# The hid of experts 8 to 14 turned by VectorE instead of TensorE, and the final rows' loads, means and squares placed anew

## The reference

```python
aff = jax.nn.softmax((xf @ w_router).astype(jnp.float32), axis=-1)
cap = EC_CAPACITY_FACTOR * n // N_EXPERTS
gate, idx = lax.top_k(aff.T, cap)
xe = xf[idx]
hid = jax.nn.silu(jnp.einsum('ecd,edf->ecf', xe, w_gate)) * jnp.einsum('ecd,edf->ecf', xe, w_up)
ye = jnp.einsum('ecf,efd->ecd', hid, w_down) * gate[..., None].astype(h.dtype)
y = jnp.zeros_like(xf).at[idx.reshape(-1)].add(ye.reshape(-1, D))
...
x = x + gate2 * rmsnorm(y, g_post_ffn)
```

## Time and profile before

| what | value |
|---|---|
| median of three runs | 2362.34 us (2360.07 to 2362.45) |
| the profiled execution, its own time | 2362.63 us |
| its span | 2360.9 us |
| TensorE's matmuls busy | 2255.7 us, 96% |
| VectorE, ScalarE, GpSimd busy | 1349.1, 1100.5, 730.6 us |
| mean DMA rate | 217 GB/s |
| granted clock of TensorE, mean | 0.988 |

### The profile page before, as it was taken

How to read it: one execution, slowest core, us unless ns; L and a number is a source line. 1 busy time by engine, 2 the same in 40 slices (tenths; PEclk the granted TensorE clock), 3 DMA queues, 4 the chain that set the end, 5 groups by cost and what they waited for, 6 DMA issues and landing times. The chain is left out here.

```text
span 2360.9 us, 34620 instructions
## 1 busy us (share of the span) xinstructions
PE 2255.7 (96%) x13219; PEld 1876.9 (79%) x13219; DVE 1349.1 (57%) x1995; ACT 1100.5 (47%) x1782; POOL 730.6 (31%) x770
## 2 busy tenths in 40 slices
PE   6999999999999999999984999999999999999997
PEld 4679989867899898677763888888888888888885
DVE  3212344555422436665557877777777667677665
ACT  4212434555534436665542544544444455545552
POOL 3004241434233515340003222221222333443634
PEclk9999999999999999999996999999999999999998
DMA  8745445657554459764538666766667678988785
GB/s 314 265 114 184 153 148 192 188 137 185 139 188 152 148 172 247 225 183 162 169 128 313 215 218 231 248 223 224 209 224 244 229 267 316 334 311 302 286 304 178
DMA packets 224095, 511.49 MB, mean 217 GB/s; under 512 B 38420, under 2 KB 129444, under 8 KB 204496
## 3 DMA queue, kind: packets, MB, share of 16 engines
q1 hardware_dynamic: 174576, 394.78, 49.3%
q0 software_dynamic: 49376, 114.78, 16.5%
HBM read 415.32 MB, written 93.69 MB: 216 GB/s over the span
## 5 line engine op out<-in xcount | busy, mean ns | idle before, releaser
L2553 DVE TENSOR_TENSOR moe_w_lo<-moe_wf,moe_w_hi 128x2048 fp32r<-128x2048 f32 x192 | 437.2, 2288 | 252.4 <-ACT moe_w_hi L2404 251.5
L2404 ACT ACTIVATE moe_w_hi<-moe_wf 128x2048 fp32r<-128x2048 f32 x192 | 366.0, 1915 | 436.7 <-PE moe_acc L2734 424.1
L2734 PE MATMUL moe_acc<-moe_w_hi,moe_x_hi 128*128 128x512 f32 x1024 | 400.1, 391 | 2.9 <-DVE moe_w_lo L2553 2.0
L2734 PE MATMUL moe_acc<-moe_w_lo,moe_x_hi 128*128 128x512 f32 x1024 | 399.2, 390 | 0.0
L2734 PE MATMUL moe_acc<-moe_w_hi,moe_x_lo 128*128 128x512 f32 x1024 | 399.1, 390 | 0.0
L2734 PEld LDWEIGHTS moe_acc<-moe_w_hi,moe_x_hi 128*128 128x128 f32 x1024 | 192.6, 188 | 43.7 <-DVE moe_w_lo L2553 2.4
L2734 PEld LDWEIGHTS moe_acc<-moe_w_hi,moe_x_lo 128*128 128x128 f32 x1024 | 192.6, 188 | 40.1
L2734 PEld LDWEIGHTS moe_acc<-moe_w_lo,moe_x_hi 128*128 128x128 f32 x1024 | 192.5, 188 | 39.7
L1793 PE MATMUL banks<-fr_w_hi,fr_h_hi 128*128 128x256 f32 x768 | 223.2, 291 | 0.0
L1793 PE MATMUL banks<-fr_w_lo,fr_h_hi 128*128 128x256 f32 x768 | 217.0, 283 | 0.0
L1793 PE MATMUL banks<-fr_w_hi,fr_h_lo 128*128 128x256 f32 x768 | 216.9, 282 | 0.0
(11 more groups left out here) (312 smaller groups left out, 4306.7 us busy)
## 6 DMA issues: line engine op xcount, KB each, us to landing
moe_wf<-in_w_expert_gate SPq DMA_DIRECT2D x64, 1024.0 KB, 5.3
moe_wf<-in_w_expert_up SPq DMA_DIRECT2D x64, 1024.0 KB, 6.0
moe_wf<-in_w_expert_down SPq DMA_DIRECT2D x64, 1024.0 KB, 6.8
fr_w_raw<-in_w_units SPq DMA_DIRECT2D x28, 1024.0 KB, 6.7
fr_bias<-in_na_bias SPq DMA_DIRECT2D x16, 1520.0 KB, 11.7
fr_a_w<-in_w_ada POOLq DMA_DIRECT2D x16, 1024.0 KB, 8.4
scratch_qk_t<-fr_stage SPq DMA_DIRECT2D x64, 256.0 KB, 2.5
scratch_vov<-fr_stage SPq DMA_DIRECT2D x96, 128.0 KB, 2.4
```

Source lines behind the costliest of these rows:

```text
L2404: nc.scalar.activation(w_hi[:, q, :, :], wf[:, q, :, :], ACT.Copy).then_inc(w_hi_ready, 1)
L2553: nc.vector.tensor_tensor(w_lo[:, q, :, :], wf[:, q, :, :], w_hi[:, q, :, :].bitcast(F32), ALU.subtract).then_inc(w_lo_ready, 1)
L2734: mm = nc.tensor.matmul(acc[:, j, b, :], x[:, g, k, :], w[:, q, a, h * HALF:(h + 1) * HALF], start=(k == 0 and i == 0), stop=(k == KC - 1 ...
```

## The change

It has five parts, all in `experts`. (1) VectorE's way of turning hid, which served experts 0 to 7, serves experts 0 to 14; TensorE turns the hid of expert 15 alone. The piece order around it is that of the early experts. (2) In GpSimd's queue the two y loads of a pair come first, without a wait; the two x1 loads follow, each behind the wait for the store of the unit two before. (3) The mean of units 0 to 25 is made by GpSimd, in front of its root, with a drain between; VectorE keeps that of unit 26. (4) The squares of a first pair stand behind down piece 1 in ScalarE's order (before: behind piece 0). (5) The squares and results of a second pair stand behind up piece 2 (before: behind piece 1).

The core of the diff (renamed semaphores, the silu's wait and most of the last expert's branch left out; down_first, turn_h and h_out stand in the code above):

```diff
-            def load_unit(n):
+            def load_y(n):
+                j = n % 2
+                g, t, e = units[n]
+                if t is not None:
+                    pool.dma_start(fy[:, j, :], y_view[t]).then_inc(fy_loaded[j], 16)
+                else:
+                    at = bass.IndirectOffsetOnAxis(ap=index_c[:, col(e, g)], axis=0)
+                    pool.indirect_dma_start(fy[:, j, :], None, io["y"], at).then_inc(fy_loaded[j], 16)
+
+            def load_x1(n):
                 j = n % 2
                 g, t, e = units[n]
                 if n >= 2:
                     pool.wait_ge(out_stored[j], 16 * (n // 2))
                 if t is not None:
-                    pool.dma_start(fy[:, j, :], y_view[t]).then_inc(fy_loaded[j], 16)
                     pool.dma_start(fx[:, j, :], x1_view[t]).then_inc(fx_loaded[j], 16)
                 else:
                     at = bass.IndirectOffsetOnAxis(ap=index_c[:, col(e, g)], axis=0)
-                    pool.indirect_dma_start(fy[:, j, :], None, io["y"], at).then_inc(fy_loaded[j], 16)
                     pool.indirect_dma_start(fx[:, j, :], None, io["x1"], at).then_inc(fx_loaded[j], 16)
...
             def root(n):
-                pool.wait_ge(y_mean, n + 1)
-                nc.gpsimd.tensor_tensor(y_r[:, n % 2:n % 2 + 1], y_ss[:, n % 2:n % 2 + 1], mhalf[:, :], ALU.pow).then_inc(y_root, 1)
+                mean = y_ss[:, n % 2:n % 2 + 1]
+                if n < LAST:
+                    pool.wait_ge(y_sq, n + 1)
+                    nc.gpsimd.tensor_scalar(mean, mean, 1.0 / D, EPS, ALU.mult, ALU.add)
+                    pool.drain()
+                else:
+                    pool.wait_ge(y_mean, n - LAST + 1)
+                nc.gpsimd.tensor_tensor(y_r[:, n % 2:n % 2 + 1], mean, mhalf[:, :], ALU.pow).then_inc(y_root, 1)
...
                     for h, half in enumerate((ns[0:2], ns[2:4])):
                         for n in half:
-                            load_unit(n)
+                            load_y(n)
+                        for n in half:
+                            load_x1(n)
...
                     split(e, DOWN, range(0, 1))
-                    if not is_late(e):
-                        h_out(e)
+                    h_out(e)
+                    split(e, DOWN, range(1, 2))
                     for n in ns[0:2]:
                         square(n)
-                    split(e, DOWN, range(1, 2))
-                    if is_late(e):
-                        turned_out(e - LATE, (h_hi, j), late_h_turned, late_h_hi_ready)
                     split(e, DOWN, range(2, NP))
 
                     silu(e + 1, 1 - j)
-                    split(e + 1, UP, range(0, 2))
+                    split(e + 1, UP, range(0, 3))
                     for n in ns[2:4]:
                         square(n)
-                    split(e + 1, UP, range(2, NP))
+                    split(e + 1, UP, range(3, NP))
...
                     split(e, DOWN, range(2, NP))
-                    for n in ns:
-                        mean(n)
-                    turned_out(e - LATE, h_hi, h_lo, j, late_h_hi_ready, late_h_ready, range(2, BK))
+                    turned_out(0, h_hi, h_lo, j, last_h_hi_ready, last_h_ready, range(2, BK))
                     for n in ns:
                         result(n)
                 else:
                     turn_x(e + 1, 1 - j)
                     split(e + 1, GATE, range(0, 2))
                     x_out(e + 1, 1 - j)
-                    if is_late(e):
-                        split(e + 1, GATE, range(2, NP))
-                        multiply(e, j)
-                    else:
-                        split(e + 1, GATE, range(2, 3))
-                        multiply(e, j)
-                        split(e + 1, GATE, range(3, NP))
-                        turn_h(e)
+                    split(e + 1, GATE, range(2, 3))
+                    multiply(e, j)
+                    split(e + 1, GATE, range(3, NP))
+                    turn_h(e)
                     split(e, DOWN, range(0, 1))
-                    if not is_late(e):
-                        h_out(e)
-                    for n in ns[0:2]:
-                        mean(n)
+                    h_out(e)
                     split(e, DOWN, range(1, 2))
-                    if is_late(e):
-                        turned_out(e - LATE, h_hi, h_lo, j, late_h_hi_ready, late_h_ready)
                     for n in ns[0:2]:
                         result(n)
                     split(e, DOWN, range(2, NP))
-                    split(e + 1, UP, range(0, 2))
-                    for n in ns[2:4]:
-                        mean(n)
+                    split(e + 1, UP, range(0, 3))
                     for n in ns[2:4]:
                         result(n)
-                    split(e + 1, UP, range(2, NP))
+                    split(e + 1, UP, range(3, NP))
...
-                    products(e + 1, GATE, 1 - j, x_hi[:, 1 - j], x_lo[:, 1 - j], first)
-                    if is_late(e):
-                        turn_h(e, j)
-                    products(e + 1, GATE, 1 - j, x_hi[:, 1 - j], x_lo[:, 1 - j], second)
-                    if is_late(e):
-                        pe.wait_ge(late_h_ready, ONE + (e - LATE) * BK + BK)
-                        products(e, DOWN, j, h_hi, h_lo)
-                    else:
-                        down_first(e, j)
-                        products(e, DOWN, j, h_hi, h_lo, range(1, NP))
+                    products(e + 1, GATE, 1 - j, x_hi[:, 1 - j], x_lo[:, 1 - j])
+                    down_first(e, j)
+                    products(e, DOWN, j, h_hi, h_lo, range(1, NP))
```

More of the change, by code:

```diff
@@ L2103, in experts @@
     FIRST, UNITS = 8, 4
-    LATE = 8
     units = [(t // TT, t, None) for t in range(GROUPS * TT)]
@@ L2184, in experts @@
         hid_ready = s.sem("hid_ready")
-        late_h_turned, late_h_hi_ready, late_h_ready = (s.sem(f"late_h_{n}") for n in ("turned", "hi_ready", "ready"))
+        last_h_turned, last_h_hi_ready, last_h_ready = (s.sem(f"last_h_{n}") for n in ("turned", "hi_ready", "ready"))
         h_turned = s.sem("h_turned")
@@ L2231, in quarter_rows @@
             return xe[:, g, :].rearrange("p (t n) -> p t n", t=4)
-        def is_late(e):
-            return isinstance(e, int) and e >= LATE
         def is_last(e, n=1):
@@ L2429, in silu @@
                     act.wait_ge(piece_done, ONE + piece(e, GATE, NP))
-                if len(bs) == BK and is_late(e - 1):
-                    act.wait_ge(late_h_turned, ONE + (e - LATE) * BK)
-                elif len(bs) == BK:
+                if len(bs) == BK:
                     act.wait_ge(h_turned, ONE + e)
@@ L2476, in body @@
                     split(e, DOWN, range(0, 2))
-                    turned_out(e - LATE, (h_hi, j), late_h_turned, late_h_hi_ready, range(0, 2))
+                    turned_out(0, (h_hi, j), last_h_turned, last_h_hi_ready, range(0, 2))
                     split(e, DOWN, range(2, NP))
@@ L2480, in body @@
                         square(n)
-                    turned_out(e - LATE, (h_hi, j), late_h_turned, late_h_hi_ready, range(2, BK))
+                    turned_out(0, (h_hi, j), last_h_turned, last_h_hi_ready, range(2, BK))
                 else:
@@ L2637, in body @@
                     split(e, DOWN, range(0, 2))
-                    turned_out(e - LATE, h_hi, h_lo, j, late_h_hi_ready, late_h_ready, range(0, 2))
+                    turned_out(0, h_hi, h_lo, j, last_h_hi_ready, last_h_ready, range(0, 2))
                     multiply(e, j, range(2, BK))
                     split(e, DOWN, range(2, NP))
-                    for n in ns:
-                        mean(n)
-                    turned_out(e - LATE, h_hi, h_lo, j, late_h_hi_ready, late_h_ready, range(2, BK))
+                    turned_out(0, h_hi, h_lo, j, last_h_hi_ready, last_h_ready, range(2, BK))
                     for n in ns:
@@ L2754, in turn_h @@
                         mm = nc.tensor.transpose(acc[:, j, b, k * P:(k + 1) * P], hid[:, b // 2, c * P:(c + 1) * P], ident[:, :])
-                    mm.then_inc(late_h_turned, 1)
+                    mm.then_inc(last_h_turned, 1)
             def down_first(e, j):
@@ L2791, in body @@
                     products(e, UP, j, x_hi[:, j], x_lo[:, j], second, bs[1])
-                    pe.wait_ge(late_h_ready, ONE + (e - LATE) * BK + 2)
+                    pe.wait_ge(last_h_ready, ONE + 2)
                     products(e, DOWN, j, h_hi, h_lo, first, bs[0])
@@ L2795, in body @@
                     products(e, DOWN, j, h_hi, h_lo, second, bs[0])
-                    pe.wait_ge(late_h_ready, ONE + (e - LATE) * BK + BK)
+                    pe.wait_ge(last_h_ready, ONE + BK)
                     for b in bs[1]:
```

1 line of the change is left out of this document (removed).

## The result

| | before | changed kernel |
|---|---|---|
| median of the runs | 2362.39 us (4 runs, 2360.07 to 2363.57) | 2417.70 us (4 runs, 2416.53 to 2419.59) |
| ratio | | 1.0237, 95% interval 1.0225 to 1.0250 |
| span of the profiled execution | 2360.9 us | 2416.5 us |

The change makes the kernel slower by 2.4%. 2355.5 us was forecast, 2363.0 was the upper end of the range: the prediction is wrong, and on the other side of no change.

The account below looks back on a forecast made before the run. TensorE and the row chain (GpSimd's queue with its DMAs) were taken as level bounds. By the row chain, -10.8, +5.8, +0.7 and -2.5 total -6.8 us from 2362.63, so 2355.8; median 2355.5 us, range 2348.5 to 2363.0.

Parts of the forecast that it names:

- The wait for the root: VectorE's results wait for GpSimd's mean, drain and root: 1.0 us for the first of a pair, 0.4 for the second.
- TensorE's sum: Experts 8 to 14 lose 16 transposes each, 12.6 us, plus one 2.0 us wait: TensorE alone ends 14.6 us earlier.
- VectorE takes the work: Each late frame gains 11.45 us of transposes on VectorE; idle time covers them, so frames 9 to 12 cost nothing.
- 1.1 us of cover: First pair, frames 9 to 12: down 2 split at +51.5, wanted by TensorE at +52.6, so no stall.
- The cover of 3.4 us: VectorE's idle time around the turn of x, taking up the some 3 us by which the second pair delays it.
- Frame 13: GpSimd late by index loads, stores and gathers: root about +68, `x_lo` +87.9, TensorE stalls 3 us.
- first rival: The row chain keeps up: y split from x1 shortens the 11 us wait, frame 13 unstalled; 2347.7 to 2352, chance 0.27.
- The row chain: GpSimd's queue with its DMAs sets the end: six frames -10.8, frame 14 +5.8, means +0.7, last loads -2.5; total -6.8 us.
- sign of being wrong: TensorE waits for splits in frames 9 to 12 (second or third rival), or TensorE ends the chain, span under 2350 us.
- The second rival: Down 2 stalls in every frame 9 to 14, VectorE awaiting roots; up to 5.6 us a pair, 2367 to 2374; chance 0.12.
- The third: Rival: stalls from VectorE's late turns of x give back six to ten of 12.6 us; 2358 to 2363, chance 0.21.
- A rule against the change: Skill puts 128 by 128 transposes on TensorE; 1.8 us of TensorE traded for 11.45 of VectorE, giving the third rival's time.

Follow-up runs that it names:

- e2: The changed kernel with the mean kept on GpSimd, but a semaphore instead of the drain between mean and root: 2357.92 us, ratio 0.9987.
- e1: The changed kernel with the mean back on VectorE for all blocks and no drain in the root: 2355.57 us, ratio 0.9973.
- e8: e1 with the second pair behind all four splits of up in frames 13 and 14 instead of three: 2354.91 us, ratio 0.9971.
- e5: e1 with the loads of y and x1 together again, as in the kernel before: 2360.94 us, ratio 0.9994.
- e4: The kernel before with only hid of experts 8 to 14 turned by VectorE; means, waits and places as before: 2380.17 us, ratio 1.0085.
- e3: The kernel before with only a drain added in the root, after its wait for the mean: 2381.53 us, ratio 1.0076.
- e7: The changed kernel, drains kept, with each pair's gather moved behind its roots and stores: 2445.90 us, ratio 1.0357.
- e9: The changed kernel, drains kept, with both groups' gathers in the first half of the frame: 2397.63 us, ratio 1.0153.

## Why the prediction was wrong, point by point

**The wait for the root** is the step that failed. It priced "a mean and a drain" at 0.4 us, from four small memsets with drains that took 0.71 us, and took 1.0 for the first and 0.4 for the second root of a pair. Those memsets stood where GpSimd had no DMA under way: its queue moves no packet between 1225 and 1240 us. Measured: 0.16 us for a drain right behind another, 0.8 to 2.1 with all packets landed, and 8.0 to 10.3 at the second pairs of the changed kernel, where it ends about 1 us behind the last packet of loads and gathers. Putting a semaphore in the drain's place, and nothing else, gives 2357.9 us (e2): 59 to 60 of the 62.2 us between forecast and result are this one term.

It could have been read. In the kernel before, line 2303 copies indices and drains, and behind two scatters the first gather comes late:

```profile
1380.88 1.48 POOL L2303 COPY moe_parts<-moe_parts 128x8 uint32 x1
1389.11 1.04 POOL L2308 DMA_INDIRECT moe_xe<-scratch_h,moe_parts  x1 [6.75 <-issue]
```

6.75 us of issue at the same copy, drain and next instruction is the nearest row, and far nearer than the memsets: the same engine with DMAs in flight. With 6.75 instead of 1.0 for the first root of each second pair, the 3 us that the second pair makes the turn of x late become 8.75, against 3.4 of idle time. That is over 5 us a frame in six frames, so by this estimate the sum comes out some 30 us higher, near 2387.

**TensorE's sum** was right: 65.3 us for a late frame (frame 8 of the changed kernel, frames 8 to 10 of e1), 1.8 us less.

**VectorE takes the work**, frames 9 to 12 at nothing: right as a walk of VectorE. e1 has 65.3 and 65.4 us in frames 9 and 10 with 55.7 and 59.1 us of work, 66.4 and 64.1 in the next two. In the changed kernel down 1 was split at +42.9 in frame 9 (the split of 1938.45 ends at 1940.73, the weighing was at 1897.83), exactly as walked. Already at that first pair the two results waited 2.9 us for their roots (2.46 and 0.44) where 1.4 was taken, more than the 1.1 us of cover beyond it, and TensorE waited 0.8 us for down 2. The cover of 3.4 us at the second pair could not hold 10. That pair, for which the forecast has no price of the root but only "some 3 us late", is where the largest waits stood.

**Frame 13** was forecast with a stall of 3 us of TensorE for `x_lo`, `x_lo` being done at +87.9. In e1 it came: 3.47 us, until +88.5 (2246.67 against 2158.19). The way there was another in part. The x1 load of unit 19 waited for no store (2216.74, +58.6 instead of +60.6), the first root stood at +65.5 instead of +68, and the two results then waited 1.2 and 2.4 us for x1 rows. So the wait of 11 us behind a store did go, as the first rival said, and the stall came all the same.

**The row chain** sets the end, as the sum had it: e8 shortened TensorE's part without the end moving. e1, which is the change less the mean on GpSimd and the drain, takes 2355.57 us; the sum was 2355.5. That close a hit is partly luck. The six frames were to give 10.8 us and give 7.3 in e1 (395.2 against 402.4), since frame 13 takes 68.6; the scatter of frame 14 was to land 5.8 us later in its frame and lands 1.2 later. Two errors of 3.5 and 4.6 us stand against each other. What follows the landing was to give 1.8 us and gives 2.1.

**The rivals.** The forecast's own sign of being wrong came, waits of TensorE for splits in frames 9 to 12. The second rival had the right engine and wait, VectorE behind a root, but its worst case was 5.6 us a pair, built from held means and roots; a drain that waits was not in it, nor was the second pair. The third gives the time of e5 (2361 us), where VectorE waits 35.5 us for squares behind late loads of y, but not of the whole change.

**A rule against the change.** The Trainium skill, VectorE: DVE Perf Modes, section Rules for kernel authors, puts 128 by 128 transposes on TensorE where PSUM will do as their destination. e4 against the kernel before agrees with it by 19 us. e5, with the new places, is level with the kernel before, and only e1, with the loads apart as well, is 6 us faster: on VectorE the transposes cost time wherever the final rows make it wait. Whether they gain any by themselves is open, for the new places and loads were not tried without them.

## What to carry to other kernels

A drain on an engine that issues DMAs is priced by what its DMA queue has in flight at that place, not by a drain where the queue is empty; order one instruction behind another on the same engine with a semaphore that the first raises. When work is moved onto an engine, walk through every wait that stands in its queue at the new fullness: waits for squares that cost nothing at 48.6 us of VectorE's work in a frame of 67.1 cost 19 us at 59 (e4). When two events bound a frame closely, price each new instruction from a row where the same instruction has the same work around it.

## What the runs showed of the chip

- A drain of GpSimd with DMAs in flight ends with its DMA queue: of 33 late roots over four kernels (the changed one, e3, e7, e9), 31 begin 0.5 to 1.2 us behind the start of the last packet of that queue, the other two 1.4 and 1.8, and a drain took up to 11.0 us (e3). A semaphore raised by the instruction before orders the same pair at no visible gap (e2).
- A mean of one column on GpSimd takes 0.19 us by itself and up to 1.67 us while VectorE works on two SBUF inputs: the mean at 1962.70 in the changed kernel lasts until 1963.75, VectorE's split of that time until 1963.70. The Trainium skill, GPSIMD Engine Reference, section Specifications, lists the SBUF interfaces as shared with VectorE, with contention for VectorE instructions with two SBUF inputs; the trace agrees.
- After waits of 3.2 to 3.6 us TensorE's matmuls ran at the 1.2 GHz level (granted clock 0.50) for 3.0 and 3.4 us in frame 10, whose matmuls took 4.0 us longer on top of 7.1 us of waits.
